# Two of four fp32 weight units behind the first norm become split units

## The reference, cut to what matters

```python
h = rmsnorm(x, attn_norm_w[l])                      # 256 x 1024
proj = h @ w_in[l]                                  # 1024 x 3592
qkv_la, z_la, b_la, a_la, q_d, k_d, v_d = jnp.split(proj, SPLIT_IDX, axis=-1)
qkv_la = jax.nn.silu(causal_conv(qkv_la, conv_w[l]))    # 4 taps along the tokens
...
```

## Time and profile before

| | |
|---|---|
| median of three runs | 748.7 us (748.19 to 749.19) |
| the profiled execution | 748.43 us |
| its span in the profile | 746.6 us |
| TensorE busy | 729.5 us, 98% of the span |
| DVE busy | 607.7 us, 81% |
| ACT busy | 441.5 us, 59% |
| moved by DMA | 147.57 MB, mean 198 GB/s |
| granted TensorE clock, mean | 1.00 |

### The profile page before, as it was taken

How to read it: one execution, slowest core, us unless ns; L and a number is a source line. 1 busy time by engine, 2 the same in 40 slices (tenths; PEclk the granted TensorE clock), 3 DMA queues, 4 the chain that set the end, 5 groups by cost and what they waited for, 6 DMA issues and landing times.

```text
span 746.6 us, 12429 instructions
## 1 busy us (share of the span) xinstructions
PE 729.5 (98%) x4680; PEld 649.8 (87%) x4680; DVE 607.7 (81%) x1038; ACT 441.5 (59%) x777; POOL 28.6 (4%) x32
## 2 busy tenths in 40 slices
PE   7999999999999999999999999999999999999996
PEld 7988999987988888888879899999888888888884
DVE  5758778777688788899898999978867888888786
ACT  5473345675655555554565557777557666666655
POOL 0031000000000000001110000000010100000000
PEclk9999999999999999999999999999999999999999
DMA  7745355544488988989616554445426555655531
GB/s 305 268 150 166 125 174 167 169 149 134 169 304 300 350 282 286 340 307 353 212 34 209 175 175 142 142 141 180 139 107 219 187 186 198 201 194 194 191 123 56
DMA packets 40380, 147.57 MB, mean 198 GB/s; under 512 B 4481, under 2 KB 4609, under 8 KB 40065
## 3 DMA queue, kind: packets, MB, share of 16 engines
q1 hardware_dynamic: 39600, 142.91, 55.8%
q10 hardware_dynamic: 722, 3.88, 1.3%
HBM read 145.72 MB, written 1.05 MB: 197 GB/s over the span
## 4 chain that ended last, share of the span: by engine, by line
PE 81%; DVE 11%; ACT 4%; issue 2%; POOL 1%; DMA 1%; DVEq 0%; ACTq 0%
PE bank L1133 18%; PE bank L1138 9%; PE bank L1191 7%; PE bank L1192 7%; PE bank L1196 6%; PE bank L1118 6%; PE bank L1121 6%; PE bank L1119 6%; PE bank L1182 3%; PE bank L1328 3%; DVE wlo L1566 3%; DVE arena L1572 2%; DVE arena L1566 2%; ACT arena L2167 2%; PE bank L1268 1%
## 5 line engine op out<-in xcount | busy, mean ns | idle before, releaser
L1566 DVE TENSOR_TENSOR wlo<-raw,whi 128x1024 fp32r<-128x1024 f32 x212 | 258.3, 1233 | 10.0 <-ACT whi L2167 9.1
L2167 ACT ACTIVATE whi<-raw 128x1024 fp32r<-128x1024 f32 x212 | 218.5, 1049 | 8.1 <-DMA raw<-w_dram 5.5
L1133 PE MATMUL bank<-hhl,whi 128*128 128x512 f32 x640 | 159.4, 391 | 0.0
L1133 PEld LDWEIGHTS bank<-hhl,whi 128*128 128x128 f32 x640 | 117.3, 188 | 22.5
L1118 PE MATMUL bank<-hhl,whi 128*128 128x256 f32 x440 | 128.4, 292 | 0.2
L1121 PE MATMUL bank<-hhl,wlo 128*128 128x256 f32 x440 | 124.4, 283 | 0.7 <-DVE wlo L1566 0.7
L1119 PE MATMUL bank<-hhl,whi 128*128 128x256 f32 x440 | 124.3, 283 | 0.0
L2167 ACT ACTIVATE arena<-bank 128x256 f32<-128x256 f32 (+2 forms) x135 | 54.9, 419 | 82.0 <-PE bank L1138 52.7
L1138 PEld LDWEIGHTS bank<-hhl,wlo 128*128 128x128 f32 x640 | 87.3, 190 | 6.2
L1138 PE MATMUL bank<-hhl,wlo 128*128 128x256 f32 x640 | 89.2, 282 | 0.0
L1118 PEld LDWEIGHTS bank<-hhl,whi 128*128 128x128 f32 x440 | 84.1, 191 | 3.8 <-issue 3.0
(11 more groups left out here) (189 smaller groups left out, 1018.2 us busy)
## 6 DMA issues: line engine op xcount, KB each, us to landing
raw<-w_dram SPq DMA_DIRECT2D x268, 512.0 KB, 4.4
arena<-rows_dram ACTq DMA_DIRECT2D x1, 1536.0 KB, 9.2
X<-x_dram SPq DMA_DIRECT2D x2, 512.0 KB, 4.2
arena<-bias_dram ACTq DMA_DIRECT2D x1, 1024.0 KB, 8.0
out_dram<-X SPq DMA_DIRECT2D x4, 256.0 KB, 2.0
const<-const_dram ACTq DMA_DIRECT2D x1, 640.0 KB, 3.9
arena<-bias_dram ACTq DMA_DIRECT2D x1, 512.0 KB, 5.8
cols<-cols_dram SPq DMA_DIRECT2D x1, 281.0 KB, 4.9
```

The lines of the kernel that those rows point to most:

```text
L1133: e.matmul(p[:, :], whi[:, s, c], hhl[:, k, :, :], start=(k == 0), stop=False)
L1566: return e.tensor_tensor(out, a, b, op)
L2167: return e.activation(out, a, func, scale=scale, **kw)
```

## The change

Of the four fp32 units only w_in 0 and 1 stay fp32. Units 2 and 3 become split units: they get `hi` and `prep` steps and are done as an ordinary pair (`cv2`) behind `conv` 0, in the loop that already does `cv4` and `cv6`.

```diff
--- before.py
+++ after.py
@@ -40,7 +40,7 @@
 def stream():
 
     units = []
-    units += [("n", "w_in", f) for f in range(4)] + [("s", "w_in", f) for f in range(4, 8)]
+    units += [("n", "w_in", f) for f in range(2)] + [("s", "w_in", f) for f in range(2, 8)]
     units += [("s", "w_in_qk", f) for f in (0, 4)]
     units += [("v", "w_in_v", u) for u in range(4)]
     units += [("s", "w_in_qk", f) for n in (1, 2) for f in (n, n + 4)]
@@ -327,20 +327,20 @@
             if n % 2 == 0:
                 P.fill(tags[n // 2], P.main % 2)
                 P.main += 1
-            i = P.unit("n", name, f, lead=3 - n)
+            i = P.unit("n", name, f, lead=len(fs) - 1 - n)
             P.of[i] = (tags[n // 2], n % 2, ("h", norm))
             ids.append(i)
-        for n in range(4):
+        for n in range(len(fs)):
             P.step("half", ids[n], 0, norm)
             if n == 2:
                 between()
-        for n in range(4):
+        for n in range(len(fs)):
             P.step("half", ids[n], 1, norm)
             if n % 2:
                 P.fills_bank(ids[n], tags[n // 2])
             else:
                 P.uses(ids[n])
-        P.need(ids[3], lead=2)
+        P.need(ids[-1], lead=2)
 
     def last_four(norm, tag, name, ks, src, block):
         ids = [P.unit("m", name, k, lead=0) for k in ks]
@@ -396,11 +396,10 @@
     for t in range(2):
         P.high((t, 0), (t, 1))
         P.low((t, 0), (t, 1))
-    halves(0, ("cv0", "cv2"), "w_in", (0, 1, 2, 3), lambda: None)
+    halves(0, ("cv0",), "w_in", (0, 1), lambda: None)
     P.step("split_ba")
     P.step("conv", 0)
-    P.step("conv", 2)
-    for f in (4, 6):
+    for f in (2, 4, 6):
         finish(pair(f"cv{f}", "w_in", (f, f + 1), ("h", 0)))
         P.step("conv", f)
     P.step("silu", 0)
```

## The result

The changed kernel takes 747.59 us (median of 22 runs, 746.81 to 748.26) against 748.99 (22 runs, 748.05 to 750.18) of the kernel before beside it. The ratio is 0.9978, with a 95% interval from 0.9972 to 0.9984: 1.65 us less, between 1.2 and 2.1. The forecast was 1.7 less; its 747.0 us started from 748.7 for the kernel before, which ran 0.3 slower in this series.

The account below looks back on a forecast made before the run. The prediction took TensorE to bound the kernel, busy 729.5 of 746.6 us, if other engines keep up. It summed -1.40 for matmuls and -0.28 for bank 0 to -1.68, forecasting 747.0 us from 748.7, range 746.1 to 748.5.

Parts of the forecast that it names:

- TensorE, removed and added: Start of the kernel: two fp32 units removed (7.16 us), two split units added (5.76 us), net -1.40 us.
- The estimate from the Trainium skill's pages: TensorE's matmul price by the skill: split unit 2.62 us, fp32 unit 3.57, so two units would save 1.90 us.
- The wait for bank 0: TensorE's hand-over from fp32 to split matmuls at `cv4`: the wait goes, -0.28 us, bounds 0 and -0.28.
- DVE, ACT, DMA at nothing: Up to `cv6`: added low halves, high halves and moved fetches cost nothing; DVE keeps 0.6 us reserve up to `cv4`.
- Behind `cv6` all moves by 1.68: After `cv6`, steps are the same on all engines, so the 1.68 us lead is carried to the end.
- the prediction's own sign: Stated test after `cv6`: the prediction is wrong if the lead at `cv6` is there and no longer at 740.
- The rival of a part given back: Behind `cv6`: shifted fetches could make a high half late, half the gain lost, 747.3 to 748.4 us; chance 0.27.
- The slower rival: Before `cv6`: unit 6 lands late and DVE stands still; 749.4 us at the slowest landing; chance 0.05.
- The rival of more than counted: TensorE behind the fp32 units: 48 added matmuls go at 0.112, not 0.12, giving 746.6 us; chance 0.08.

Follow-up runs that it names:

- the order alone: Against the kernel before: units 2 and 3 stay fp32 but are done as a second pair behind conv 0; ratio 0.9993, first fp32 matmul to first `ba` 25.81 us.
- late taps: Changed kernel with DVE writing the low halves of units 6, 7 and 8 once more, to a place nobody reads; ratio to the kernel before 1.0012.
- halves early: Kernel before with one fp32 unit; unit 1 split, its halves ahead of the activations' split, low-part matmuls last; ratios 0.9964 and 0.9961.
- turned buffers: Changed kernel with every unit's high and low halves in the buffer of the kernel before (slot numbers turned by three); one run, 748.27 us.
- no fp32 unit: Kernel before with all units split, none in fp32; ratio to the kernel before 1.0059, median 753.25 us.

## Why the prediction was right

**TensorE, removed and added: -1.40.** Right to 0.01 us: it is the difference between the order alone and the change, 25.81 and 24.41. The spacing of 0.12 that the sum used holds for the added matmuls too (from 18.24 to 35.39 there are 143 spacings of 0.120). The estimate from the Trainium skill's pages, 1.90, is refuted by that row.

**The wait for bank 0: -0.28.** Right in kind, too small: it was 0.41. I let the fp32 group end one whole record behind its last start, while the split matmul can follow after 0.03.

**DVE, ACT, DMA at nothing.** Right. Taken 0.99 later, the taps and low halves came out within 0.15 of their places, and 0.55 us were left of the 0.6 to spare. ACT waited for no fetch behind `cv0` (its three high halves started at 19.05, right behind the scalings), and unit 6 was fetched at 16.53, as laid out.

**Behind `cv6` all moves by 1.68.** Half right. The lead there was 1.81, and all of it reached 165; then ACT's gap took back 0.25. At 700 us the three profiles of the changed kernel are ahead of the first one of before by 1.46, 1.61 and 1.53, counted from the start of their fp32 matmuls, and of the second one of before by 0.09 less; the runs say 1.65 (1.2 to 2.1), and can't tell these numbers apart. By the prediction's own sign, a lead at `cv6` that is no longer there at 740, it was wrong by these 0.25 us. That the total is met so closely is in part luck: the sum had 0.13 too little for the bank and nothing for the gap's 0.25, and the two nearly offset each other. The rival of a part given back came true in small, with 0.25 us and not half of the gain, and through a place in ACT's instruction stream, not through a late fetch, as I had it.

**The slower rival** did not occur, but its mechanism is real: in the kernel with late taps the same queue, 3.4 us longer, made the kernel slower than before. That run lengthened DVE's work; no landing was late enough to do the same, and ACT's waits of 2.18 and 0.24 us for unit 6 (halves early, late taps) didn't delay `ba`. The rival of more than counted was wrong in its cause: the added matmuls went at 0.120 and not at 0.112. There was 0.13 more than counted, at the bank.

## What to carry to other kernels

Units done in a dearer form ahead of a split are there to cover the splitting: price the exchange by what TensorE would find waiting, not by the matmuls alone. Here the exchange of two units of four, with their new place in the order, took 1.8 us off d, and no other step had to be moved for it. The exchange of a third took nothing off (0.09 was added), and 0.7 with its halves moved forward and its matmuls reordered. For a change of 0.2%, compare the time between two landmarks around the edit, since the start of a profile wanders by a microsecond. It repeated to 0.01 us between profiles of one kernel, except where the slow pace of the start reached past the first landmark (24.65 for 24.41 with turned buffers, below).

## What the runs showed of the hardware

- The start wanders. In thirteen profiles the first fp32 matmul lies between 9.92 and 11.16. Two things add up: the x tile was there for DVE at 4.58 before and 5.08 after, and the turns took 2.83 and 3.26 us. The stretch from 9 to 10 us of the two first profiles, before and then after, has 11 and 6 matmuls in it:

```profile
9.00:10.00 1.00, 1.00 (x11) 1.00 (x10) 0.85 (x3) 0.64 (x1) 0.00 (x0) 1.00 1.02 418
```

```profile
9.00:10.00 1.00, 1.00 (x6) 1.00 (x6) 0.80 (x2) 0.24 (x1) 0.00 (x0) 1.00 1.04 418
```

- The slow part goes at the pace of the lower clock. The turns start 0.21 us apart and then, from one matmul to the next, 0.11 apart; the step comes at 9.1 us before and at 10.6 after. That is nearly the ratio that the split matmuls show between a granted clock of 0.50 and of 1.00 (0.21 and 0.12, no fp32 unit). The clock's column (behind POOL's) has 1.00 in both rows above, but the records of the clock in the traces begin only at 9.13 and 10.57 us, with an entry of 1.00, so ahead of them the column rests on nothing. In all fourteen profiles the step lies at that first record, which comes between 8.50 and 11.65 us. That the clock stood at 1.2 GHz before it is inferred from the pace; no record says so. In the profile with turned buffers the first record comes last of all, at 11.65, and the slow pace reaches into the fp32 matmuls, which start at 11.16. They take 7.55 us for 7.31, and d is 24.65:

```profile
11.00:12.00 1.00, 1.00 (x8) 1.00 (x7) 0.84 (x2) 0.68 (x2) 0.00 (x0) 1.00 1.04 418
12.00:13.00 1.00, 1.00 (x12) 1.00 (x11) 1.00 (x3) 0.87 (x2) 0.00 (x0) 1.00 1.03 414
```

- An idle stretch of 4.73 us on TensorE brought its granted clock from 1.00 (2.4 GHz) to 0.50 (1.2 GHz), from about 12 to 18.7 us, four of them at work. That cost 1.8 us beside the idle time itself. The Trainium skill, "TensorE: Matmul & The Clock Gate", section "HAM oscillation — how this bites in real kernels", tells of TensorE waiting between bursts and starting each at half clock; the trace agrees.
- Two more high halves in ACT's stream, in its first 35 us, opened a gap of 0.25 us in front of an instruction at 165, and one small instruction more closed it again. What makes it is open.
